# A hybrid decoder step on one core: last two turns' rows added by TensorE, other rows combined meanwhile, sample rows spread, weights tabled

## What is computed

```python
h = rms_norm(x, norm_ffn)                       # N = 528 prompt and meta rows, 8 sample rows, 1024 wide
g = argmax over 4 groups; top 2 of the 8 experts in that group
gates[n, e] = softmax over the two * g_probability
y = jnp.zeros((N, 1024), float32)
for e in range(32):
    act = silu(h @ w_gate[e]) * (h @ w_up[e])   # 1024 -> 256
    y = y + gates[:, e:e+1] * (act @ w_down[e]) # 256 -> 1024
x = x + y
y_prompt = rms_norm(x, norm_final)[:, 16:]      # 512 rows; y_sample: 8 rows
```

## Time and profile before

| | us |
|---|---|
| Median of 3 runs | 689.49 |
| Lowest and highest | 686.68 to 692.34 |
| The profiled execution | 690.71 |
| Its span | 689.0 |
| PE busy in it | 608.1 (88%) |
| DVE, ACT, POOL busy | 279.4, 139.4, 116.2 |
| HBM read, written | 150.91 MB, 19.01 MB |

### The profile page before, as it was taken

One profiled execution on the slowest core, in us unless ns is written; L12 is line 12 of the kernel. 1 busy time (PEld: TensorE's weight loads), 2 busy tenths in 40 slices (PEclk: granted clock), 3 DMA queues, 4 the chain that ended last, 5 costly groups with the idle time before them and its releaser, 6 DMA issues.

```text
span 689.0 us, 8590 instructions
## 1 busy us (share of the span) xinstructions
PE 608.1 (88%) x3171; PEld 330.1 (48%) x3171; DVE 279.4 (41%) x615; ACT 139.4 (20%) x407; POOL 116.2 (17%) x195
## 2 busy tenths in 40 slices
PE   4999999999999999999989996999999977999700
PEld 2444444444544555555545573655555543555300
DVE  3320059433234452668788777412112111121146
ACT  3110142333333454311131100110101000011112
POOL 2341007220040110101030101021111210111023
PEclk9999999999999999999999955999999998999955
DMA  9626156833030300041084798999999999999774
GB/s 293 214 74 187 37 179 201 279 111 123 1 94 29 115 8 1 0 123 63 1 324 185 227 409 345 392 418 418 418 421 418 422 422 420 421 419 421 306 262 170
DMA packets 49378, 161.45 MB, mean 234 GB/s; under 512 B 16443, under 2 KB 17772, under 8 KB 36664
## 3 DMA queue, kind: packets, MB, share of 16 engines
q1 hardware_dynamic: 39624, 143.67, 53.9%
q0 software_dynamic: 7488, 17.19, 7.5%
q10 hardware_dynamic: 2224, 0.04, 0.2%
HBM read 150.91 MB, written 19.01 MB: 247 GB/s over the span
## 4 chain that ended last, share of the span: by engine, by line
PE 68%; DMA 13%; SPq 9%; DVE 4%; ACT 3%; issue 2%; POOL 1%; POOLq 0%; DVEq 0%; ACTq 0%
PE bank L1883 13%; PE bank L1880 12%; PE bank L2101 8%; PE scores L2166 5%; PE bank_p L2153 5%; DMA WS<-in_w_down_e 5%; DMA XHT<-in_w_down_e 4%; SPq L556 3%; PE bank_t L2153 3%; SPq L553 3%; PE bank_t L1897 3%; SPq L550 2%; DMA WS<-in_w_in 2%; PE bank_p L2006 2%; PE scores L2023 1%
## 5 line engine op out<-in xcount | busy, mean ns | idle before, releaser
L1883 PE MATMUL bank<-WS,XHT 128*128 128x512 f32 x192 | 91.7, 626 | 2.6 <-DMA WS<-in_w_in 2.1
L1880 PE MATMUL bank<-XHT,WS 128*128 128x512 f32 x192 | 85.0, 597 | 0.6 <-PE bank_t L1897 0.6
L1883 PEld LDWEIGHTS bank<-WS,XHT 128*128 128x128 f32 x192 | 36.5, 199 | 46.0 <-issue 43.0
L1880 PEld LDWEIGHTS bank<-XHT,WS 128*128 128x128 f32 x192 | 35.7, 190 | 42.8 <-issue 42.6
L2153 PE MATMUL bank_p<-WS,XHT 128*64 128x256 f32 x288 | 45.7, 392 | 4.5 <-DMA FT<-in_w_up_e 1.2
L916 POOL DMA_INDIRECT out_rows<-MVA,slot_ids x17 | 17.0, 1002 | 185.0 <-DVE MVA L1748 185.0
L2153 PE MATMUL bank_t<-WS,XHT 128*64 128x256 f32 x288 | 42.9, 381 | 0.2 <-DVE XHT L1731 0.2
L2153 PEld LDWEIGHTS bank_p<-WS,XHT 128*64 128x64 f32 x288 | 27.8, 141 | 19.2 <-issue 4.7
L1748 DVE COPY MVA<-scores 128x512 f32<-128x512 f32 x17 | 11.8, 692 | 56.0 <-PE scores L2166 56.0
L2153 PEld LDWEIGHTS bank_t<-WS,XHT 128*64 128x64 f32 x288 | 27.2, 137 | 13.3 <-DMA FT<-in_w_up_e 0.4
L807 POOL TENSOR_SCALAR rr<-ss 128x1 f32<-128x1 f32 (+3 forms) x25 | 7.5, 301 | 152.2 <-ACT XHT L1150 42.9
(11 more groups left out here) (428 smaller groups left out, 1014.8 us busy)
## 6 DMA issues: line engine op xcount, KB each, us to landing
WS<-in_w_gate_e SPq DMA_DIRECT2D x16, 1024.0 KB, 19.1
WS<-in_w_up_e SPq DMA_DIRECT2D x16, 1024.0 KB, 20.8
WS<-in_w_down_e SPq DMA_DIRECT2D x16, 1024.0 KB, 25.3
WS<-in_w_in SPq DMA_DIRECT2D x6, 2048.0 KB, 10.7
XHT<-in_w_gate_e SPq DMA_DIRECT2D x10, 1024.0 KB, 23.2
XHT<-in_w_up_e SPq DMA_DIRECT2D x10, 1024.0 KB, 25.9
XHT<-in_w_down_e SPq DMA_DIRECT2D x10, 1024.0 KB, 28.4
FT<-in_w_gate_e SPq DMA_DIRECT2D x6, 1024.0 KB, 22.5
```

What stands on the lines that cost most here:

```text
L1880: mm = pe.matmul(PS[r][:, :], w[:, k, 128 * m:128 * (m + 1)], hT[:, k, 0:512], start=(k == 0), stop=(k == KC - 1))
L1883: mm = pe.matmul(PS[r][:, :], hT[:, k, 128 * m:128 * (m + 1)], w[:, k, :], start=(k == 0), stop=(k == KC - 1))
```

## The change

**The last two turns** (`ENDING`: turns 15 and 16). Their rows stay in the two `YO` buffers, and TensorE adds them to the tokens: for each of tiles 0 to 3 a matrix `chosen[k]` (128 slots by 512 tokens, the routing weight where slot and token belong together, 0 elsewhere) times the rows, both turns accumulated in eight PSUM banks (`late`, 16 matmuls of 128x512). ScalarE evacuates both halves of turn 16.

**`chosen`** is made ahead. SyncE writes the weights `pw` to a table in HBM ordered by partition (`pw_rows`) in the load loop's fifth pair; VectorE works out each slot's place in it (`choose`, 20 small instructions, after turn 2's work); GpSimd fetches the weights from it by two indirect DMAs of 128x1 and makes masks (`few_masks`, after turn 3's `store`); VectorE forms the two matrices (`choose_weights`, in turn 7).

**`out_rows`** no longer gets the last two turns' rows, which GpSimd scatters to a second tensor, `end_rows`. So a token's row may be missing: SyncE writes zeros over the prompt's part of `out_rows` and the samples' part of both, ahead of the experts' first loads, from `maskneg`, which GpSimd sets to zero after the last `decay`.

**Read-back.** SyncE waits for turn 14's down product and for the scatters up to turn 14, and then issues for tiles 0 to 3 the x rows and both read-backs. VectorE adds these (`gather_early`) to new buffers `XE`, and the PSUM banks behind it (`add_late`). The wait of SyncE for `all_out` now stands ahead of the samples' read-back alone. VectorE, ScalarE and SyncE wait for scatters of turns 15 and 16 no more, except through it; GpSimd's waits, its `all_out` and its roots stand as before.

**The samples** are laid over 128 partitions, 16 for each, 64 columns in each (`spread`); their square sums are added by a matmul with a block matrix (`alike`), their weights and norm factors laid out alike (`pick`, `gfew`). They are combined between tiles 2 and 3 (`LASTLY`). TensorE loads the count ahead of the last `dn`.

```diff
-LASTLY = (T4, 0, 1, 2, 3)
+LASTLY = (0, 1, 2, T4, 3)
...
+ENDING = (STATIC - 2, STATIC - 1)
...
-        out_rows = dram("out_rows", (2 * SECOND, D))
+        out_rows, end_rows = dram("out_rows", (2 * SECOND, D)), dram("end_rows", (2 * SECOND, D))
+        pw_rows = dram("pw_rows", (128 * 2 * NTILES, 1))
...
+                    sp.wait_ge(sel_made, 2)
+                    for c in range(2):
+                        sp.dma_start(out_rows[SECOND * c:SECOND * c + SEQ].rearrange("(p r) (b d) -> p (r b) d", p=128, d=128),
+                                     maskneg[:, None, :].to_broadcast([128, 32, 128])).then_inc(rows_zeroed, 16)
+                        for rows in (out_rows, end_rows):
+                            sp.dma_start(spread(rows, SECOND * c + SEQ + S0), maskneg[:, 0:64]).then_inc(rows_zeroed, 16)
...
+                if n == 2 * NSETS:
+                    for b in range(NDEC):
+                        sp.dma_start(gfew[16 * b:16 * b + 16], norm_final.rearrange("(s d) -> s d", d=64)).then_inc(gfin_in, 16)
+                if n == NSETS + 1:
+                    sp.wait_ge(ids_ready, 2)
+                    sp.dma_start(pw_rows.rearrange("(p n) a -> p (n a)", p=128), pw[:, :, :].rearrange("p c j -> p (c j)"))\
+                      .then_inc(pw_out, 16)
                 sp.wait_ge(dn_filled, LAST[n - NSETS] + 1)
                 for u in range(2):
...
-            sp.wait_ge(dn_filled, LAST[PAIRS - 2] + 1)
-            for j in range(NTILES):
-                n = nrows(j)
-                sp.dma_start(X[0:n, j, :], x_rows[128 * j:128 * j + n]).then_inc(x_back[j], 16)
...
+            sp.dma_start(XE[T4], spread(x_rows, SEQ + S0)).then_inc(x_back[T4], 16)
+
+            sp.wait_ge(dn_filled, LAST[PAIRS - 3] + 1)
+            for s in range(2):
+                sp.wait_ge(y_out[s], 16 * ((ENDING[0] + 1 - s) // 2))
+            for j in range(NT):
+                sp.dma_start(XE[j], x_rows[128 * j:128 * (j + 1)]).then_inc(x_back[j], 16)
+                for c in range(2):
+                    sp.dma_start(YG[j][:, c], out_rows[SECOND * c + 128 * j:SECOND * c + 128 * (j + 1)])\
+                      .then_inc((x_back, y_in)[c][j], 16)
 
             sp.wait_ge(all_out, 1)
-            src = out_rows.rearrange("(c t) d -> t c d", c=2)
-            for c in range(2):
-                sp.dma_start(YG[T4][S0:N4, c], src[SEQ + S0:SEQ + N4, c]).then_inc((x_back, y_in)[c][T4], 16)
-            for j in range(NT):
+            for n, rows in enumerate((out_rows, end_rows)):
                 for c in range(2):
-                    sp.dma_start(YG[j][:, c], src[128 * j:128 * (j + 1), c]).then_inc((x_back, y_in)[c][j], 16)
...
+                    sp.dma_start(y_prompt[0, 128 * j:128 * (j + 1), 512 * half:512 * half + 512],
+                                 XE[j][:, 512 * half:512 * half + 512]).then_inc(fin_out, 16)
...
+                    if h == H - 1:
+                        pool.wait_ge(mixed, len(UNITS))
+                        link(pool.memset(maskneg[:, :], 0.0))
+                        pool.nop().then_inc(sel_made, 1)
...
-                pool.indirect_dma_start(out_rows, bass.IndirectOffsetOnAxis(ap=slot_ids[:, c, 1:2].bitcast(u32), axis=0),
+                pool.indirect_dma_start(end_rows if i in ENDING else out_rows, bass.IndirectOffsetOnAxis(ap=slot_ids[:, c, 1:2].bitcast(u32), axis=0),
...
+            def few_masks():
...
+                link(pool.memset(pick, 0.0))
...
+                link(pool.iota(column_int, [[1, 512]], base=0, channel_multiplier=0))
+                link(pool.tensor_copy(column, column_int))
+                link(pool.memset(pw_end, 0.0))
+                pool.nop().then_inc(sel_made, 1)
+                pool.wait_ge(pw_out, 16)
+                pool.wait_ge(chosen_made, 1)
+                for k, i in enumerate(ENDING):
+                    pool.indirect_dma_start(pw_end[:, k:k + 1], None, pw_rows,
+                                            bass.IndirectOffsetOnAxis(ap=place_end[:, k:k + 1].bitcast(u32), axis=0),
+                                            bounds_check=128 * 2 * NTILES - 1, oob_is_err=False).then_inc(pw_in, 16)
+                link(pool.memset(alike[:, :], 1.0))
...
+                pool.nop().then_inc(sel_made, 1)
...
+            pool.wait_ge(rows_zeroed, 16 * 6)
             for i in range(STATIC):
                 if i + 3 < STATIC:
                     fetch(i + 3)
                 store(i)
+                if i == 3:
+                    few_masks()
...
             pool.nop().then_inc(all_out, 1)
             for k, j in enumerate(LASTLY):
-                n = nrows(j)
-                rsqrt(rr[0:n, 10 + j:11 + j], ss[0:n, 10 + j:11 + j], D, fsq, k + 1)
+                rsqrt(rr[:, 10 + j:11 + j], ss[:, (15 if j == T4 else 10 + j):][:, 0:1], D, fsq, k + 1 + (k >= LASTLY.index(T4)))
...
+                if i == STATIC - 1:
+                    copy(YO[s][:, 512:1024], Sps[:, 0, 512:1024]).then_inc(y1, 1)
...
-                    act.wait_ge(fsq, k)
-                act.activation(junk2[0:n, :], X[0:n, j, :], ACT.Square,
-                               accum_out=ss[0:n, 10 + j:11 + j]).then_inc(fsq, 1)
+                    act.wait_ge(fsq, k + (k > LASTLY.index(T4)))
+                act.activation(junk2[:, 0:XE[j].shape[1]], XE[j], ACT.Square, accum_out=ss[:, 10 + j:11 + j]).then_inc(fsq, 1)
+                if j == T4:
+                    act.wait_ge(few_filled, NT + 2)
+                    copy(ss[:, 15:16], bank[0][:, 0:1]).then_inc(fsq, 1)
...
+            def choose():
+
+                for k, i in enumerate(ENDING):
+                    out_id, place, part = slot_ids[:, TURNS[i][1], 1:2], place_end[:, k:k + 1], part_end[:, k:k + 1]
+                    link(v.tensor_scalar(place, out_id, 127, None, ALU.bitwise_and))
...
+                    ins = v.tensor_tensor(place, number[:, 3:4], number[:, 2:3], ALU.add)
+                    link(ins) if k == 0 else ins.then_inc(chosen_made, 1)
+
+            def choose_weights():
+
+                dve.wait_ge(sel_made, 3)
+                dve.wait_ge(pw_in, 32)
+                for k, i in enumerate(ENDING):
+                    link(v.tensor_copy(id_end[:, k:k + 1], slot_ids[:, TURNS[i][1], 0:1]))
+                    v.tensor_scalar(chosen[k], column, id_end[:, k:k + 1], pw_end[:, k:k + 1],
+                                    ALU.is_equal, ALU.mult).then_inc(chosen_made, 1)
+
+            def gather_early(j):
+
+                dve.wait_ge(x_back[j], 32)
+                for c in range(2):
+                    if c:
+                        dve.wait_ge(y_in[j], 16)
+                    link(v.scalar_tensor_tensor(XE[j], YG[j][:, c], pw[:, c, j:j + 1], XE[j], ALU.mult, ALU.add))
+
...
+            def add_late(j):
...
+                dve.wait_ge(few_filled, j + 2)
...
+                    ins = v.tensor_tensor(XE[j], XE[j], Sps[:, j - 2, :], ALU.add)
+                ins.then_inc(x2_ready, 1)
...
+            def gather_few():
...
+                dve.wait_ge(x_back[T4], 16)
+                dve.wait_ge(y_in[T4], 64)
+                for n in range(4):
+                    ins = v.scalar_tensor_tensor(XE[T4], Yfew[:, n], pwfew[:, n % 2:n % 2 + 1], XE[T4], ALU.mult, ALU.add)
...
             def finish(k):
 
                 j = LASTLY[k]
-                r = slice(0, 128) if j < NT else slice(S0, N4)
                 dve.wait_ge(rsq, 4 * NTILES + k + 1)
...
-                    v.scalar_tensor_tensor(X[r, j, c], X[r, j, c], rr[r, 10 + j:11 + j], gfin[r, c],
...
+                for c in ((slice(0, 64),) if j == T4 else (slice(0, 512), slice(512, D))):
+                    v.scalar_tensor_tensor(XE[j][:, c], XE[j][:, c], rr[:, 10 + j:11 + j], gfew if j == T4 else gfin[:, c],
                                            ALU.mult, ALU.mult).then_inc(yfin, 1)
...
+                if i == STATIC - 1:
+                    dve.wait_ge(few_filled, 1)
+                    v.tensor_copy(pwfew, Sps[:, 1, 0:2])
...
-            second_half(STATIC - 1)
+                if i == 2:
+                    choose()
+                if i == NSETS + 4:
+                    choose_weights()
...
-
-            for s in range(2):
-                dve.wait_ge(y_out[s], 16 * ((STATIC + 1 - s) // 2))
-            further(dve, further_blocks(dve), further_pair)
...
+            further(dve, further_blocks(dve), further_pair, stored=all_out)
+            gather_early(0)
+            gather_early(1)
+            add_late(0)
+            gather_early(2)
+            add_late(1)
+            finish(0)
+            gather_early(3)
+            add_late(2)
+            finish(1)
+            gather_few()
+            add_late(3)
+            for k in range(2, NTILES):
+                finish(k)
...
                 gate_up(PS["t" if s else "p"], xT[s], w, 32 * (n // NSETS) + 32, 2 * i + 1)
+                if i == STATIC - 1:
+                    pe.wait_ge(sel_made, 2)
```

(32 more changed lines are left out.)

111 lines of the change are left out of this document (68 added, 43 removed).

## The result

| | before | after |
|---|---|---|
| Median, us | 689.45 (16 runs) | 683.71 (16 runs) |
| Lowest and highest | 686.68 to 696.51 | 679.14 to 688.75 |
| Ratio, 95% interval | | 0.9916, 0.9893 to 0.9939 |
| Span of the profiled execution | 689.0 | 683.6 |
| HBM written | 19.01 MB | 23.34 MB |

The changed kernel is 5.7 us or 0.8% faster. The forecast was 684.6 us, a gain of less than 1%.

A forecast was written before the change was run, and what follows sets the result against it. A 41 us tail behind the weight stream, with idle DMA engines and VectorE, was the target: 5.6 us saved there, less 0.7 in the stream, is 4.9 off 689.49, giving 684.6 us; range 680.5 to 688.5.

The forecast's parts named there:

- What bounds the kernel, and the read-back: Tail of 41 us after the weight stream leaves DMA engines idle; read-backs issued from 642.5 to 648.7 fill it.
- The gate: GpSimd's inverse roots still wait for both last scatters; tile 0's scaling starts at 666.3, after VectorE has stood 4.5 us.
- VectorE ahead of the gate: In the tail VectorE starts at 650.4, sums tile 0 by 657.4 and tile 1 by 661.8, before GpSimd's root.
- TensorE's late matmuls: 16 f32 matmuls of 128x512 behind turn 16's down product: 7.1 us, 14.3 at the lower clock, costing nothing.
- The scatter's landing: Last scatter, issued at 655.85 into full DMA engines, takes 8.0 us and lands at 663.85.
- lands at once: Rival: last scatter takes 4.4 us instead of 8.0, first scaling at 662.7, time 681.0; chance 0.22.
- The end: From tile 3's sum at 675.2, square, root, scaling and output landing keep their 8.2 us, ending at 683.4.
- The zeroing: Writing 4.33 MB of zeros to `out_rows` ahead of the experts' loads takes 10 to 19 us, ends by 341, costs nothing.
- The rival at 701 us: Zero writes run into the experts' first loads; at 71 GB/s they end at 383, kernel slower; chance 0.05.
- The stream: Small transfers inside the expert-weight stream, some 640 packets, cost 0.7 us, charged in full.
- signs of being wrong: Scatter under 5 us without idle stretch, VectorE waiting for read-backs or TensorE, or stream's end moved over 2 us.
- The sum: Tail 5.6 us shorter, less 0.7 for small transfers in the weight stream: net gain 4.9, time 684.6.

The follow-up runs named there:

- the late read-back: Changed kernel, but SyncE waits for `all_out` ahead of all read-backs, as before the change: 700.59 us against 695.63 before, ratio 1.007.
- half the read-back: Changed kernel without the second read-back of tiles 0 to 3, the first used twice: 682.83 us; with tile 0's root also ahead of GpSimd's scatter waits, 680.86 us.
- the samples-third run: Changed kernel with tile 0's root ahead of scatter waits, eight norm-weight loads ahead of the stream, samples third in the last norm: 685.01 us, ratio 0.9843.
- the small loads early: Changed kernel with the eight loads of the samples' last-norm weights moved from inside the weight stream to ahead of it: 688.28 us, ratio 0.9892.
- the second profile: Changed kernel run once more, unedited, in a later comparison: 684.33 us, ratio 0.9931.
- the zeros twice: Changed kernel with the two 2 MB zero writes made again, to a tensor nothing reads: 689.53 us, ratio 0.9912.

## Why the prediction came out right, and what in it was wrong

**What bounds the kernel, and the read-back: right.** The idle DMA engines of the tail were the thing to fill; the late read-back loses it all. Issue was foreseen from 642.5 to 648.7, and was from 643.75 to 652.0: turn 14's scatter was issued 1.7 us later by the trace's clock (635.30) and landed after 8.40, and the last issues were slower (2.92 us for two), which I had not foreseen.

**The gate: its time right, its role wrong.** The forecast had VectorE at tile 0's scaling at 661.8 and the root at 666.3, a stall of 4.5 us. From turn 14's down product (628.35 before) that is 33.45 and 37.95. Measured: the root's end allowed 35.6 at full clock and 37.5 at the lower one, which is the clock of the profile that the sum was made from. So at like clock the gate was sized within half a microsecond. What failed is the step "VectorE ahead of the gate": it gets there at 35.9 to 36.2 us, 2.5 us later than worked out. Tile 0's rows are in at 23.3 instead of 22.05; the last weights, issued ahead of them, came only at 20.7 (650.75, where turn 16's down product waits for them), and the forecast had them in by 648. Tile 1 comes 1.7 us behind VectorE's first pair instead of 0.2; at the lower clock 0.95 more goes to TensorE's late matmuls, which I had called covered and priced at half: 14.0 us at the full clock, not 7.1. A stall of 4.5 us shrank to one of 1.3 or to none. At the lower clock the gate still sets tile 0's scaling, so its time carried the end. At the full clock the sum fits by luck: VectorE came 2.5 us later than worked out and the root 2.4 us sooner, and they met near 36.

**The scatter's landing: a little too long.** 8.0 us was taken for the last scatter. It took 6.7 to 6.9 at the full clock and 7.5 at the lower one with all rows and read-backs, 5.7 and 4.6 with half the read-back, and 2.8 with the read-backs late. The rival "lands at once" falls. The page "DMA: Bandwidth & Descriptors" of the Trainium skill (section "Queues, rings and completion order") let me estimate 4.4 for a loaded landing; under full engines the runs show 6.7 to 7.5, so they do not bear this estimate out. Its fit for a lone transfer, 2.0 us and bytes over 436 GB/s (section "Anatomy of one DMA — SWDGE (gpsimd) path"), gives an estimated 3.2 for 0.52 MB. But the late read-back's last two scatters moved 0.17 and 0.21 MB, for which it gives an estimated 2.4 and 2.5; they landed after 3.5 and 2.8, 1.1 and 0.3 us more than that. The 0.52 MB for each of them in the forecast's queue were too much by 0.3 to 0.35.

**The end: right.** 8.2 us from tile 3's sum to the end were taken, 8.8 measured (674.78 to 683.6). Most of the 0.6 is the samples' root, which stands in front of tile 3's on GpSimd; the samples-third run takes 0.4 of it away. Tile 3's sum was foreseen at 675.2, and came at 674.78 by the trace's clock; from turn 14's down product that is 46.85 foreseen and 44.73 measured (46.26 at the lower clock, with the small loads early).

**The zeroing: right.** In by 340 (foreseen 341), at 262 to 346 GB/s; twice as much is hidden too. The rival at 701 us falls.

**The stream: right by the windows.** 0.7 us were charged, 0.9 are missing between 465 and 530. The last weights went out 2.6 us later than before in the first profile, which is among the forecast's signs of being wrong. But 3.2 us of delay arose ahead of the stream, where the clock fell; in the second profile, without that, they went out 299.54 us behind the load of `dec_mk`, and 299.19 before. GpSimd's fetch moved from 487.62 to 494.93, as foreseen, and nothing waited for it.

**The sum.** At like clock the tail is 60.65 - 55.1 = 5.5 us shorter, with 5.6 foreseen (55.1 is of the runs with the small loads early and with the zeros twice; the changed kernel itself has no profile of that kind); the first profile's 7.1 holds 1.6 us of clock. With 0.7 to 0.9 for the stream that leaves 4.6 to 4.8. That the first profile's span, 683.6, is so near the 683.4 of the forecast is luck: it gained 2.8 us ahead of the load of `dec_mk` (318.55 for 321.38), lost 4.5 from there to turn 14's down product, and gained 7.1 behind it. The two ratios of the changed kernel, 0.9916 and 0.9931, are 5.8 and 4.8 us.

## What to carry to other kernels

Where a tail waits for a read-back that needs only most of the scattered rows, split off the last ones, and the read-back can go out under the stream; then look for the second and third limit before removing the first, since here three lay within 1.5 us and no edit alone gave more than 1.8 us in the tail. Price an instruction by what the trace shows for one instruction of the program: two records can stand for one matmul. A sum can come out right over a stall that is not there: ask of each wait in it how early the waiting engine arrives, not only when the gate opens. When executions spread by more than the effect, measure from an event that all kernels share, and sort the traces by the clock first.

## What the runs showed of the hardware

- The same eight matmuls (16 records) behind the same wait for weights took 3.65 us in seven profiles and 5.2 to 5.4 in seven others; the granted clock was 1.00 in the one kind; in the other its lowest window of 5 us had 0.66 to 0.81. What decides between them stays open: TensorE was busy 2.88 of 5 us ahead of it before and 3.87 after, but 3.00 in the second profile of the kernel after, which kept the full clock.
- A 128x512 matmul in f32 with 128 rows of weights stood in the trace as two records 0.43 us apart at the full clock: 16 of them took 14.0 us.
- A scatter by 128 indices, most of them out of bounds, moved 0.17 or 0.21 MB. It landed after 3.5 and 2.8 us with little beside it (DMA share 0.16 and 0.20, its own bytes included), and after 7.4 and 6.9 beside twelve half-megabyte loads; without its payload it landed only 0.5 us sooner.
- Zero writes in packets of 512 bytes moved 262 to 346 GB/s at a share of 0.89 to 1.15 of the DMA engines. Before, the 256-byte store reached 142 at 0.63, by proportion an estimated 225 at a full share.
- Eight loads of 4 KB each, inside a stream that kept a share of 1.02, took it from 419 to 413 GB/s over 65 us.
- On GpSimd a multiply by a column over 128x1024 in f32 took 3.38 us and an addition 2.34; one fused pass on VectorE takes 1.28.
